# Expert routing without GpSimd arithmetic, 96 candidate pairs a head, and head norms with one reciprocal

## The reference

```
# first block: o has 4 heads of 128;  third block: 8 heads;  delta rule of the second block: 4 heads
o = o * rsqrt(mean(o * o, -1) + eps)          # per head and token, then gain and gate
# second block: q and k, 4 heads of 128 each
q = q * rsqrt(sum(q * q) + eps) * 128 ** -0.5;   k = k * rsqrt(sum(k * k) + eps)
# second block, experts: 8 heads, 2 x 128 keys a head, 16384 experts
v1, i1 = top_k(s1, 16);  v2, i2 = top_k(s2, 16)
cand = v1[:, None] + v2[None, :]              # 256 pairs a head
score, pos = top_k(cand, 16)                  # 16 experts a head, 128 a token
ids = i1[pos // 16] * 128 + i2[pos % 16];  gates = softmax(score)
out = sum(gates * gelu(h . expert_u[ids]) * expert_v[ids])
```

## Time and profile before

| | |
|---|---|
| median of three runs | 4513.59 us |
| the profiled execution | 4514.63 us |
| its span | 4512.9 us |
| TensorE busy / VectorE / ScalarE / GpSimd | 84% / 60% / 26% / 12% |
| granted TensorE clock, mean | 0.918 of 2.4 GHz |
| the up projections of the experts | 2009.0 to 2701.7 us |
| the down projections | 2716.4 to 3288 us |

### The profile page before, as it was taken

How to read it: one execution, slowest core, us unless ns; L and a number is a source line. 1 busy time by engine, 2 the same in 40 slices (tenths; PEclk the granted TensorE clock), 3 DMA queues, 4 the chain that set the end, 5 groups by cost and what they waited for, 6 DMA issues and landing times. The chain is left out here.

```text
span 4512.9 us, 50869 instructions
## 1 busy us (share of the span) xinstructions
PE 3787.8 (84%) x18835; PEld 3223.6 (71%) x18835; DVE 2688.0 (60%) x3850; ACT 1178.9 (26%) x1989; POOL 562.7 (12%) x381
## 2 busy tenths in 40 slices
PE   7998966799976556799899998999968877679998
PEld 6876753588755346579889898999946837556876
DVE  4444777444345565439999967777743447564433
ACT  1101123211031201113377773333321112322300
POOL 0000021000000020001456662222200000000000
PEclk9999978899988868899999999999979988889999
DMA  3222700222212000225888789999912102011232
GB/s 139 98 72 83 271 15 1 100 93 74 77 38 83 0 6 1 89 76 183 290 271 284 281 303 325 329 328 322 319 53 89 56 21 75 2 65 62 96 98 70
DMA packets 198406, 590.97 MB, mean 131 GB/s; under 512 B 22336, under 2 KB 80704, under 8 KB 196040
## 3 DMA queue, kind: packets, MB, share of 16 engines
q1 hardware_dynamic: 161368, 454.46, 29.2%
q0 software_dynamic: 36864, 134.23, 8.4%
HBM read 536.19 MB, written 52.43 MB: 130 GB/s over the span
## 5 line engine op out<-in xcount | busy, mean ns | idle before, releaser
L332 DVE CAST w_hi<-w_ring 128x1024 fp32r<-128x1024 f32 (+1 forms) x336 | 238.6, 710 | 642.4 <-PE banks L297 493.7
L71 DVE TENSOR_TENSOR w_lo<-w_ring,w_hi 128x1024 fp32r<-128x1024 f32 (+1 forms) x336 | 424.6, 1264 | 11.5
L297 PE MATMUL banks<-x_hi,w_hi 128*128 128x512 f32 x896 | 355.8, 397 | 48.2 <-DVE x_lo L71 47.4
L1803 PE MATMUL up_ps<-h_hi,u_hi 128*128 128x384 f32 x1024 | 358.5, 350 | 35.8 <-DVE u_lo L71 35.6
L2083 PE MATMUL out_ps<-w_hi,v_hi 128*128 128x384 f32 x1024 | 346.8, 339 | 42.3 <-DVE w_lo L71 42.3
L297 PE MATMUL banks<-x_lo,w_hi 128*128 128x512 f32 x896 | 354.1, 395 | 0.0
L297 PE MATMUL banks<-x_hi,w_lo 128*128 128x512 f32 x896 | 353.9, 395 | 0.0
L1803 PE MATMUL up_ps<-h_lo,u_hi 128*128 128x384 f32 x1024 | 349.3, 341 | 0.0
L1803 PE MATMUL up_ps<-h_hi,u_lo 128*128 128x384 f32 x1024 | 348.8, 341 | 0.0
L2083 PE MATMUL out_ps<-w_hi,v_lo 128*128 128x384 f32 x1024 | 345.4, 337 | 0.0
L2083 PE MATMUL out_ps<-w_lo,v_hi 128*128 128x384 f32 x1024 | 345.3, 337 | 0.0
(11 more groups left out here) (495 smaller groups left out, 8113.5 us busy)
## 6 DMA issues: line engine op xcount, KB each, us to landing
expert_tiles<-peer_u SPq DMA_DIRECT2D x128, 512.0 KB
expert_tiles<-peer_v SPq DMA_DIRECT2D x128, 512.0 KB
w_ring<-w_in SPq DMA_DIRECT2D x104, 512.0 KB, 3.7
w_ring<-ffn_up SPq DMA_DIRECT2D x88, 512.0 KB, 3.4
w_ring<-w_ff SPq DMA_DIRECT2D x64, 512.0 KB, 3.7
ada_ring<-w_ada SPq DMA_DIRECT2D x48, 512.0 KB, 5.4
peer_acts<-act_ring SPq DMA_DIRECT2D x128, 192.0 KB
peer_gates<-staging SPq DMA_DIRECT2D x12, 2048.0 KB, 11.1
```

The lines of the kernel that those rows point to most:

```text
L71: return nc.vector.tensor_tensor(self.lo[at], value, self.hi[at].bitcast(F32), ALU.subtract)
L297: last = nc.tensor.matmul(banks[:, j, s, 0:n], a[:, u % 2, k, :], b[:, g * kg + k, x_from + c:x_from + c + n], start=(g == 0 and k == 0 an ...
L332: nc.vector.tensor_copy(w_parts.hi[:, u % 2], ring[:, u % slots]).then_inc(hi_ready, 1)
L1803: last = nc.tensor.matmul(up_ps[:, n % 3, 0:DENSE], a[:, n % 2, k, :], b[:, k, P:T], start=(k == 0 and part_ == 0), stop=(k == DB - 1 and ...
```

## The change

- **GpSimd only issues gathers** in `experts_up`. The multiplies by the tables of key numbers go to VectorE as route steps of their own (five steps follow step 41 of a chunk, where there were three), in a tile `hit` of their own, and `hits` and `weights` are gone with their semaphores.
- **Gated one-hot rows**: for each token of a group, one operation with two pointer scalars, equal to the key, times the gate, 128x128; four a group in place of one 128x512 on VectorE and one on GpSimd.
- **96 candidates**: of the 16x16 pair sums of two falling lists only rows 0 and 1 in full, 8 of rows 2 and 3, and 4 of rows 4 to 15 are made, by three adds. A position among 96 is decoded by a shift, a minimum, a shift of a mask and an and; the first key comes from a sum of differences of neighbouring key numbers over the rows that begin at or before the position.
- **The table**: the phases have 14, 9, 32, 27, 25 and 19 tiles (16, 9, 27, 26, 26 and 22 before), with 38, 28, 30 and 32 dots in the last four (38, 30, 30, 30), and a chunk's last steps come together ahead of the next chunk's, where they were interleaved.
- **Head norms**: a class `HeadRows`. The sum of head b is put on partition b by a matmul with a strip of zeros that has a one in column b, all heads into one bank of [heads, 512]; then one root, one reciprocal of [heads, 512], and one matmul a head with a selector that spreads row b over 128 partitions into PSUM, where VectorE reads it. A first small root loads ScalarE's table ahead of the squares. The scalings of q and k are folded in. In the first block `kv_ps` has three banks of four, and the fourth head waits for one.

```diff
-            kv_ps = p.ps(c2, "kv_ps", [P, 4, 4, P])
+            kv_ps = p.ps(c2, "kv_ps", [P, 3, 4, P])
...
+            norm_rows = HeadRows(p, c2, H, RMS_EPS, 1.0 / P, kd[0:H, 1, 0:H * P + T])
...
+                    if h == 3:
+                        pe.wait_ge(state_ready, NC - 1)
...
-                    nc.tensor.matmul(kv_ps[:, h].rearrange("p a t -> p (a t)"), p.ones, sq[:, h * T:h * T + T],
-                                     start=True, stop=True).then_inc(summed, 1)
+                    norm_rows.sum(pe, h, sq[:, h * T:h * T + T])
+                pe.wait_ge(state_ready, H * (NC - 1))
+                for h in range(H):
+                    if h == 3:
+                        pe.wait_ge(gated, 1)
+                    norm_rows.spread_to(pe, h, kv_ps[:, h % 3].rearrange("p a t -> p (a t)"))
...
+                norm_rows.invert(dve)
                 for h in range(H):
                     sl = slice(h * T, h * T + T)
-                    dve.wait_ge(rms_ready, h + 1)
-                    nc.vector.reciprocal(rms[:, sl], rms[:, sl]).then_inc(normed, 1)
-                    dve.wait_ge(normed, 2 * h + 1)
-
-                    nc.vector.tensor_tensor(gate[:, sl], gate[:, sl], rms[:, sl], ALU.mult).then_inc(normed, 1)
-                    dve.wait_ge(normed, 2 * h + 2)
+                    dve.wait_ge(norm_rows.spread, h + 1)
+                    nc.vector.tensor_tensor(gate[:, sl], gate[:, sl], kv_ps[:, h % 3].rearrange("p a t -> p (a t)"), ALU.mult) \
+                        .then_inc(gated, 1)
+                    dve.wait_ge(gated, h + 1)
                     nc.vector.scalar_tensor_tensor(out=mix[:, h, :], in0=o_ps[:, h, :], scalar=norm_g[:, h:h + 1],
...
+class HeadRows:
+    def __init__(self, p, ctx, nb, eps, scale, room=None):
+        self.p, self.nb, self.eps, self.scale = p, nb, eps, scale
+        self.strip = p.sb(ctx, "strip", [P, 2 * nb - 1])
+        room = p.sb(ctx, "head_rows", [nb, nb * P + T])[:] if room is None else room
+        self.sel, self.root = room[:, 0:nb * P].rearrange("a (b m) -> a b m", b=nb), room[:, nb * P:nb * P + T]
+        self.eps_col = p.sb(ctx, "eps_col", [nb, 2])
+        self.sums = p.ps(ctx, "sums", [nb, T])
+        self.prepared, self.summed, self.rooted, self.inverted, self.spread = p.sems(
+            ctx, "prepared", "summed", "rooted", "inverted", "spread")
+    def prepare(self, dve):
+        nc, nb = self.p.nc, self.nb
+        nc.vector.memset(self.eps_col[:], self.eps).then_inc(self.prepared, 1)
+        nc.vector.memset(self.strip[:], 0.0).then_inc(self.prepared, 1)
+        dve.wait_ge(self.prepared, 2)
+        nc.vector.memset(self.strip[:, nb - 1:nb], 1.0).then_inc(self.prepared, 1)
+        nc.vector.tensor_copy(self.sel, over(self.p.ident[0:nb, 0:nb].unsqueeze(2), [nb, nb, P])).then_inc(self.prepared, 1)
+    def warm(self, act):
+        act.wait_ge(self.prepared, 1)
+        self.p.nc.scalar.activation(self.eps_col[:, 1:2], self.eps_col[:, 0:1], ACT.Sqrt)
+    def sum(self, pe, b, square):
+        if b == 0:
+            pe.wait_ge(self.prepared, 4)
+        self.p.nc.tensor.matmul(self.sums[:], self.strip[:, self.nb - 1 - b:2 * self.nb - 1 - b], square,
+                                start=(b == 0), stop=(b == self.nb - 1)).then_inc(self.summed, 1)
+    def take_root(self, act):
+        act.wait_ge(self.summed, self.nb)
+        self.p.nc.scalar.activation(self.root, self.sums[:], ACT.Sqrt, bias=self.eps_col[:, 0:1], scale=self.scale) \
+            .then_inc(self.rooted, 1)
+    def invert(self, dve):
+        dve.wait_ge(self.rooted, 1)
+        self.p.nc.vector.reciprocal(self.root, self.root).then_inc(self.inverted, 1)
+    def spread_to(self, pe, b, bank):
+        pe.wait_ge(self.inverted, 1)
+        self.p.nc.tensor.matmul(bank, self.sel[:, b, :], self.root, start=True, stop=True).then_inc(self.spread, 1)
...
+            for b in range(nb + 1):
+                if b < nb:
+                    factor = gain[b] if isinstance(gain, tuple) else gain[:, b:b + 1]
+                    dve.wait_ge(rows.spread, b + 1)
+                    nc.vector.scalar_tensor_tensor(out=o[:, b, :], in0=o[:, b, :], scalar=factor, in1=banks[:, b % 4, :],
+                                                   op0=ALU.mult, op1=ALU.mult).then_inc(scaled, 1)
+                if b and gate is not None:
+                    dve.wait_ge(scaled, b)
+                    nc.vector.tensor_tensor(dst[:, b - 1, :], o[:, b - 1, :], gate[:, b - 1, :], ALU.mult).then_inc(gated, 1)
...
-            head_norm(p, qkv[:, 0:8, :], None, p.unit_gain, qk, 8, 1, eps=RMS_EPS / P)
+            head_norm(p, qkv[:, 0:8, :], None, (float(P) ** -0.5,) * 4 + (1.0,) * 4, None, 8, scale=1.0)
...
-                    nc.vector.tensor_scalar(q, qk[:, 0:4, :], 1.0 / P, None, ALU.mult).then_inc(scaled, 1)
-                    nc.vector.tensor_scalar(k, qk[:, 4:8, :], float(P) ** -0.5, None, ALU.mult).then_inc(scaled, 1)
...
-    MIDDLE = [2.6] + [0.85] * 4 + [1.0] * 8 + [0.85] * 4 + [1.0] * 4 + [3.9]
-    COSTS = {"route": HEAD + MIDDLE + [4.6, 2.3, 1.1], "gate": [0.72] * GROUPS, "dot": [1.3] * SLOTS}
+    MIDDLE = [1.8] + [0.5] * 4 + [0.65] * 8 + [0.5] * 4 + [0.65] * 4 + [4.2]
+    COSTS = {"route": HEAD + MIDDLE + [2.3, 4.6, 2.3, 2.3, 1.1], "gate": [1.15] * GROUPS, "dot": [1.3] * SLOTS}
...
-        (16, route(0, 0, TAIL)),
+        (14, route(0, 0, TAIL)),
...
+        (32, beside(route(1, 18, TAIL) + handover(1, 0, 18), steps("dot", 0, 0, 38))),
+        (27, beside(beside(route(2, 18, TAIL) + handover(2, 0, 12), steps("gate", 1, 0, GROUPS)), steps("dot", 0, 38, 66))),
+        (25, beside(beside(route(3, 12, TAIL) + route(3, TAIL, STEPS), steps("gate", 2, 0, GROUPS)), steps("dot", 0, 66, 96))),
+        (19, beside(steps("gate", 3, 0, GROUPS), steps("dot", 0, 96, SLOTS)))]
...
-            def hits(c, j):
-
-                pool.wait_ge(hit_made, 2 * c + j + 1)
-                i2 = idx_f[:].rearrange("p (h two) k -> p h two k", two=2)
-                nc.gpsimd.tensor_tensor(hit, hit, over(i2[:, :, j, :].unsqueeze(2), [P, H, K, K]), ALU.mult) \
-                    .then_inc(hit_weighed, 1)
-
-            def weights(g):
-                c, at = g // GROUPS + 1, g % GROUPS * GROUP_TOKENS
-                pool.wait_ge(row_ready, g + 1)
-                nc.gpsimd.tensor_tensor(gated[:, g % HOTS], gated[:, g % HOTS],
-                                        over(picks[:, c % 2, 2, at:at + GROUP_TOKENS].unsqueeze(2), [P, GROUP_TOKENS, NKEYS]),
-                                        ALU.mult).then_inc(weights_ready, 1)
...
+                for at, first, rows, width in ((0, 0, 2, K), (32, 2, 2, 8), (48, 4, 12, 4)):
+                    shape = [P, H, rows, width]
+                    then(nc.vector.tensor_tensor(
+                        cand[:, :, at:at + rows * width].rearrange("p h (a b) -> p h a b", a=rows),
+                        over(v2[:, :, 0, first:first + rows].unsqueeze(3), shape),
+                        over(v2[:, :, 1, 0:width].unsqueeze(2), shape), ALU.add))
...
+                     nc.vector.tensor_tensor(row_diff[:, :, 1:], i1[:, :, 1:], i1[:, :, 0:K - 1], ALU.subtract))
...
+                then(nc.vector.tensor_scalar(part[:, 0], pos[:], 4, None, ALU.logical_shift_right))
+                settled()
+                then(nc.vector.tensor_scalar(part[:, 0], part[:, 0], 3, None, ALU.min))
+                settled()
+                then(nc.vector.tensor_tensor(part[:, 1].rearrange("p h k -> p (h k)"), row_mask[:],
+                                             part[:, 0].rearrange("p h k -> p (h k)"), ALU.logical_shift_right))
+                settled()
+                then(nc.vector.tensor_tensor(part[:, 1].rearrange("p h k -> p (h k)"),
+                                             part[:, 1].rearrange("p h k -> p (h k)"), flat_pos, ALU.bitwise_and),
+                     nc.vector.tensor_copy(part_f[:, 0], pos[:]))
...
-                for j in range(2):
-                    nc.vector.tensor_tensor(flat, over(part_f[:, j].rearrange("p h k -> p (h k)").unsqueeze(2), [P, H * K, K]),
-                                            over(iota[:, 0:K].unsqueeze(1), [P, H * K, K]), ALU.is_equal).then_inc(hit_made, 1)
+                then(nc.vector.tensor_copy(part_f[:, 1], part[:, 1]))
+                settled()
+                i2 = idx_f[:].rearrange("p (h two) k -> p h two k", two=2)[:, :, 1, :]
+                flat = hit[:].rearrange("p h k a -> p (h k) a")
+                for j, (marks, relation, table) in enumerate(((row_start[:], ALU.is_ge, row_diff[:]), (iota[:, 0:K], ALU.is_equal, i2))):
+                    then(nc.vector.tensor_tensor(flat, over(part_f[:, j].rearrange("p h k -> p (h k)").unsqueeze(2), [P, H * K, K]),
+                                                 over(marks.unsqueeze(1), [P, H * K, K]), relation))
                     yield
-                    dve.wait_ge(hit_weighed, 2 * c + j + 1)
```

(13 more changed lines are left out.)

134 lines of the change are left out of this document (50 added, 84 removed).

## The result

The changed kernel takes **4438.4 us** in the median of 4 runs (4433.3 to 4444.7), the kernel before 4517.2 in the same session. The ratio is 0.9828, with a 95% interval of 0.9802 to 0.9853: 79 us faster. The forecast was 4428, range 4395 to 4476, faster with a chance of 0.92. The time lies in the range, 10 us above the forecast.

What follows compares the result with a forecast made beforehand. VectorE was taken to bound the expert stage's pieces from 2079.0 to 2570.6 us, TensorE the others, with serial head-norm reciprocals the second place. 4513.6 - 47 (expert stage) - 38.5 (head norms) = 4428 us, range 4395 to 4476.

Steps and rivals of the forecast that it cites:

- The expert stage: Stage of all experts' up projections: 645 us against 693, -47 us, with the bound moving from VectorE to TensorE in middle pieces.
- The 11 us that I had added for bursts: Pieces of 32, 27 and 25 tiles: TensorE needs 407 us, VectorE 391; tiles with a long operation add 11, making 418.
- the price of 0.25: Gated one-hot: each of four 128x128 operations costs 0.25 us, so 96 x (1.0 - 0.68) = +31 us of VectorE.
- the last piece: Piece of 19 tiles: TensorE needs 108 us, but 39 MB of transfers at 345 GB/s take 113; 114 was taken.
- The head norms: Four norms, fewer reciprocals: q/k -12.5, first block -6.4, four heads -3.5, eight heads -16; together -38.5 us.
- my bounds of -46 and -33: Head norms' gain in us with all TensorE spreads at the full clock (-46) or all at half (-33).
- Gathers stop scalar operations: Rival, expert stage: each GpSimd gather holds up VectorE's one-hot operations 1.02 us; 4474 us; chance 0.10.
- The upper price: Rival, gated one-hot: each short operation costs 0.49 us, 92 us more of VectorE; 4467 us; chance 0.05.
- Transfers: Rival: transfers become the bound from the 32-tile piece on, 586 us at 285 GB/s, +54; 4482 us; chance 0.08.
- All at its floor: Rival: bursts cost nothing and spreads run at full clock; stage -66, norms -46; 4402 us; chance 0.10.
- Stretch from elsewhere: Rival: something other than GpSimd's multiply stretches VectorE's operations, so 74 us stay; 4485 us; chance 0.03.
- Slower: Rival: a gather holds a scalar operation up to 1.98 us, at all 90 gathers from the first group; 4560 us; chance 0.04.

Runs made afterwards that it cites:

- the second profile: The changed kernel run once more, unaltered, against the kernel before: 4440.6 us (0.9829); its profiled execution took 4431.4.

## Why the prediction was right, and where it was off

**The expert stage**, forecast -47, measured -54 in one profile and -52 in the other; the same stage code in four more kernels gave -53, -51, -51 and -45.
- The pieces: 62 forecast and 62.1 measured; 41 and 39.2; 418 and 141.1 + 140.4 + 136.8 = 418.3; 114 and 108.3; 10 and 10.3. The bound moved to TensorE in the middle pieces. The 11 us that I had added for bursts were a guess; 8 of them came in one piece, that of 32 tiles, so that the sum fits to 0.3 us is luck.
- The stretched operations went back to 1.22 and 1.21 us, as forecast, and two runs show that GpSimd's multiply was the cause.
- The multiplies cost 2.28 us each, as forecast (2.29). The candidate passes fell from 62.0 to 35.0 us busy, -27 for the forecast -29.
- The gated one-hot is busy 1.09 to 1.34 us a group and 1.19 in the mean. Start to start, as the prediction counts, the four stand 0.26 us apart and a group takes 1.03 in the median, so the price of 0.25 was right. The term was still too small: it took a whole duration, 0.68, off a sum counted start to start. Counted one way, 1.03 less 0.60 is +41 us; the other way, 1.19 less 0.68, it is +49; I had +31. It hardly showed, since VectorE's busy time in the three middle pieces, 394.9 us, stayed under their 418. The price of the form was nearer to the equal size than to the bound of 0.49. The section on the errata in *VectorE: DVE Perf Modes* of the Trainium skill speaks for long tiles; here two operations of 512 lost to four of 128, and my reading, which no run tests, is that it is because each of the four does both steps.
- The step that failed was the last piece: I had 114 us from a transfer rate of 345 GB/s, and it took TensorE's 108. The rate was right (343 GB/s), the need was not: I had counted all that the piece issues, 39 MB, and 343 GB/s over 108.3 us is 37. The error was 6 us, and without it the stage's sum is 639. In the five other profiles of this stage the piece took 108.5 to 111.7 us.

**The head norms**, forecast -38.5, of which each end measured: first block, from its sums to its last product, 22.3 to 16.0 us, -6.3 (forecast -6.4); q/k, from the block's start, -7.9 (-12.5); four heads -1.3 (-3.5); eight heads -12.8 (-16). The sum is -28, outside my bounds of -46 and -33. Three steps failed; the reciprocal was none of them, it cost its 3.34 us once, as forecast.
- The spreads of q/k: I took four of eight at full clock, and all 16 passes stayed at half, 14.0 us for 10.2. That is 3.8 us.
- The first spread of the two gated norms: I had taken off the reciprocals and added a late start and slower spreads, but VectorE's first product also waits for a whole spread before it, 2.1 us (1788.8 to 1790.9, and 3656.2 to 3658.3), which my sum put at nothing. The root itself starts 4.9 and 5.3 us later than before, where I had 4 to 5.
- The sums: 9.95 us for 9.09, 6.34 for 5.40 and 8.73 for 7.13, and an unchanged 3.60 in the first block. I had taken them as unchanged.

The last two are why the gain fell below even my bound of -33, which had all spreads at half clock. Why the sums are slower is open. The table load ahead of the squares makes TensorE's idle time before them longer (6.5 us for 5.1, 3.3 for 1.9, 3.1 for 1.8), and in the first block, where TensorE does not idle, nothing changed. But in all eleven profiles with the new norms that idle time is the same to 0.3 us, and the q/k sums took 9.8 to 10.0 us in seven of them and 8.3 to 8.7 in four, those of four heads 6.3 to 6.6 and 3.6 to 5.3. The idle time alone does not set it; that a sum now fills 4 or 8 rows of its bank and not 128 is another difference, which no run tests by itself.

**The sum.** -54 and -28 make -82; the profile shows -73, the second profile -83. In the first, what lies around the norms ahead of the expert stage gave back 4 us, the down projections 4, and the stages between them and the last norm 2. Against the forecast that is +10 by the norms, +10 by what came back and -7 by the expert stage, which leads from 4428 to the 4441 of this execution. That the total missed by only 10 us is in part luck: the parts missed by more, in opposite directions.

**The rivals.** *Gathers stop scalar operations*: of 384 of them, the 56 over 0.4 us all lie beside a gather. The clearest case, four operations with a gather and four without:

```profile
2259.96 1.33 DVE L2017 TENSOR_SCALAR gated<-iota,picks 128x128 f32<-128x128 f32 x4
2260.30 0.94 POOL L1636 DMA_INDIRECT gathered<-peer_u_rows,expert_ids  x1 [3.01 <-DVE gathered L1643]
...
2261.33 1.09 DVE L2017 TENSOR_SCALAR gated<-iota,picks 128x128 f32<-128x128 f32 x4
```

Here the gather costs its group 0.24 us, in the mean of the 69 groups beside one 0.12 us, and not the 1.02 of the rival; 168 more of the 384 operations ran beside a gather and took no more than 0.4 us. *SBUF: State Buffer* of the Trainium skill, "Who interferes with whom", states that tensor_scalar in a two-port mode and GpSimd lock each other out for a whole instruction. This trace does not show that length: the longest operation took 0.55 us beside a gather of 0.94. Whether the few longer ones are that lock in part is not shown; that it happened at all I had not expected from the cast of the earlier trace rows. *The upper price* of 0.49 us fell with the 0.26. *Transfers*: the last full piece has 0.94 of the DMA engines busy, and its dots waited 16 us for rows, but TensorE only 1.3. *All at its floor* held for the pieces of 27 and 19 tiles, not for that of 32, nor for the spreads. *Stretch from elsewhere* fell with two experiments. *Slower* had no part of it.

The three signs that I had named for being wrong were all there in small, and none took the time out of the range: VectorE's short operations stretch beside a gather, by 0.12 us a group; 29.3 us of idle time before the dots are put down to gathered rows; and a spread takes 1.71 us, just over the 1.7.

## What to carry to other kernels

When GpSimd computes beside VectorE, price it by what it stretches, not by its own idle time; giving the gates' multiply to VectorE paid here, 15 us, even though VectorE had little to spare. When a change moves the bound to a second engine within 4% of the first, expect part of whatever is added to the first: here 14 of 25 us showed. In the kernel before, whose bound was VectorE in two pieces, 17 of 43 us freed came back as time. And a norm that hands its rows to TensorE must price TensorE at half clock after an idle time such as the 4 us here, and count the first spread that VectorE waits for. Keeping TensorE busy with five useless products took 10 to 12 us off the norms in the traces, and 16 off the time, give or take 11.
